# Writing out the routing stage of a mixture-of-experts layer, with its token lists built by one-hot products

## The reference

```python
x = x + mixed @ w_out[l]
h2 = rms_norm(x, norm_ffn_g[l])
...
group_p = jax.nn.softmax((ht @ rg_w + rg_b).astype(jnp.float32), axis=-1)
gp, gi = lax.top_k(group_p, 1)
...
tp, ti = lax.top_k(ep, TOP_K)
...
order = jnp.argsort(flat_e)
...
padded = ((counts + MOE_BLOCK - 1) // MOE_BLOCK) * MOE_BLOCK
...
dest = pstart[se] + (jnp.arange(A, dtype=jnp.int32) - start[se])
...
slot_tok = jnp.full((cap,), T, jnp.int32).at[dest].set(stok)
...
xb = h_pad[slot_tok].reshape(n_blocks, MOE_BLOCK, D)

def expert_block(args):
    xblk, e = args
    hid = jax.nn.silu(xblk @ w1[e]) * (xblk @ w3[e])
    return hid @ w2[e]
```

## Time and profile before

| | us |
|---|---|
| median of 3 timed runs | 4951.96 (4951.84 to 4953.2) |
| the profiled execution, as a whole | 4939.51 |
| span of its trace, first to last instruction | 4937.7 |
| PE busy in it | 4243.3 (86%) |
| DVE / ACT / POOL busy | 1567.0 / 1090.8 / 290.2 |

### The profile page before, as it was taken

The page is one execution under the profiler, slowest core; times in us unless marked ns, Lnnn a source line. Parts: engine busy times, 40 slices in busy tenths (PEclk is TensorE's granted clock), DMA queues, the critical chain, the costliest instruction groups (busy, mean ns, idle before and its releaser), DMA issues. The chain is left out here.

```text
span 4937.7 us, 63014 instructions
## 1 busy us (share of the span) xinstructions
PE 4243.3 (86%) x23058; PEld 2190.4 (44%) x23059; DVE 1567.0 (32%) x2896; ACT 1090.8 (22%) x1837; POOL 290.2 (6%) x297
## 2 busy tenths in 40 slices
PE   7899996888987849984988969999969995999996
PEld 4555445774433424442444534444434443444442
DVE  3355463542221122223165530110136536100112
ACT  1155223442100101111044300000026522000002
POOL 0000002320000010001000000000000000000000
PEclk9899998999998869997999979999989997999998
DMA  2130145432213139975001458888731133888884
GB/s 90 54 143 24 49 162 135 89 68 77 93 35 115 64 128 370 357 265 208 17 14 72 173 185 311 304 309 313 247 112 43 64 112 131 304 313 309 311 305 174
DMA packets 427020, 820.70 MB, mean 166 GB/s; under 512 B 146640, under 2 KB 288080, under 8 KB 393808
## 3 DMA queue, kind: packets, MB, share of 16 engines
q1 hardware_dynamic: 397968, 717.33, 41.9%
q0 software_dynamic: 17216, 60.83, 4.3%
q10 hardware_dynamic: 11648, 39.88, 2.0%
HBM read 692.09 MB, written 125.86 MB: 166 GB/s over the span
## 5 line engine op out<-in xcount | busy, mean ns | idle before, releaser
L2829 PE MATMUL ec1e_pg<-ec_wg,ec1e_xT 128*128 128x512 f32 x1024 | 445.2, 595 | 2.2 <-DVE ec1e_xT L2882 2.2
L2829 PE MATMUL ec0e_pg<-ec_wg,ec0e_xT 128*128 128x512 f32 x1024 | 444.5, 595 | 2.1 <-DVE ec0e_xT L2882 2.1
L2829 PEld LDWEIGHTS ec1e_pg<-ec_wg,ec1e_xT 128*128 128x128 f32 x1024 | 195.6, 191 | 249.0 <-issue 249.0
L2829 PEld LDWEIGHTS ec0e_pg<-ec_wg,ec0e_xT 128*128 128x128 f32 x1024 | 195.4, 191 | 248.3 <-issue 248.3
L1371 PE MATMUL mix_pb<-h_h_all,mix_wg 128*128 128x512 f32 x512 | 223.3, 597 | 12.2 <-DMA mix_wg<-in_w_in_dram 12.2
L1861 PE MATMUL exp_pg<-exp_wb,exp_xT 128*128 128x512 f32 x512 | 224.9, 598 | 6.4 <-DMA exp_wb<-in_w_dram 6.4
L3113 PE MATMUL lrui_pA<-lrui_xT,lrui_w 128*128 128x512 f32 x512 | 223.1, 595 | 2.6 <-ACT lrui_xT L3187 2.6
L2855 PE MATMUL ec1e_py<-lru_wd,ec1e_hidT 128*128 128x512 f32 x512 | 223.4, 594 | 0.0
L2855 PE MATMUL ec0e_py<-gqaw_wd,ec0e_hidT 128*128 128x512 f32 x512 | 223.4, 594 | 0.0
L679 PE MATMUL front_pz<-h_h_all,front_w 128*128 128x512 f32 x480 | 211.6, 599 | 8.8 <-DMA front_ones<-in_head_ones_dram 8.8
L2190 PE MATMUL gqap_pq<-gqap_w,gqap_xT 128*128 128x512 f32 x384 | 180.7, 631 | 22.4 <-DVE gqap_xT L2235 17.5
(11 more groups left out here) (533 smaller groups left out, 6135.5 us busy)
## 6 DMA issues: line engine op xcount, KB each, us to landing
ec_wg<-in_moe_w_gate_up_dram SPq DMA_DIRECT2D x256, 1024.0 KB, 6.4
exp_wb<-in_w_dram SPq DMA_DIRECT2D x64, 1024.0 KB, 15.2
gqaw_wd<-in_moe_w_down_dram SPq DMA_DIRECT2D x128, 512.0 KB, 4.4
lru_wd<-in_moe_w_down_dram SPq DMA_DIRECT2D x128, 512.0 KB, 4.4
exp_w2b<-in_w_dram SPq DMA_DIRECT2D x32, 1024.0 KB, 14.2
wkv_inp<-arrays SPq DMA_DIRECT2D x160, 128.0 KB, 3.0
arrays<-front_out SPq DMA_DIRECT2D x36, 512.0 KB, 5.7
yb<-mlaa_zero SPq DMA_DIRECT2D x1, 16384.0 KB, 52.8
```

Of the source, the lines that this page charges most:

```text
L2829: return nc.tensor.matmul(pg[:, b, :], xT[:, k, :], wg[:, k, b * HALF:(b + 1) * HALF], start=k == 0, stop=k == KD - 1)
```

## The change

Routing is written out, without loops, for all 8 tiles. `po`, `x1`, `xt`, `h2` and `h2T` exist twice and alternate by tile. The product is issued in halves with the transposes and logits of the tile before between them; the residual sum too is made in halves, each released by its own count. `mT` goes into the products directly. `mT`'s first part, `wo` and the first `x` tiles are loaded ahead of the constants. The choice of experts is made for tiles 0 to 5 inside the written-out sequence, and for tiles 6 and 7 after it.

The list of tokens is no longer scattered. For each of the 16 columns of slots DVE makes two one-hot arrays: `at_pos` (position in the block, 128 wide) and `in_block` (number of the block, 48 wide, times the token's number). 16 products on PE sum them to `pt[position, block]`, which is the list, and DVE copies it to `moe.idx`. As soon as the experts of blocks 0 and 1 are known SP loads their weights, and POOL gathers their rows, both still inside the routing phase. Buffers that both phases use belong to a new outer phase `moe`. In the experts loop SP loads the weights of the second pair of a turn and of the first pair of the next turn; POOL copies a column of `moe.idx` before each gather.

The core of the diff:

```diff
+class Moe:
...
+        self.idx = ph.sb("idx", [P, MOE_BLOCKS + 2], U32)
+        self.block_e = ph.sb("block_e", [P, MOE_BLOCKS + 2], U32)
+        self.pair_used = ph.sb("pair_used", [P, MOE_BLOCKS // 2 + 1], U32)
+        self.xg = ph.sb("xg", [P, self.R, D])
+        self.wb = [ph.sb("wb0", [P, 2, 2, KD, D_EXP]), None]
+        self.w2b = [ph.sb("w2b0", [P, 2, 2, D]), None]
+        self.wg_done = [ph.sem(f"wg_done{s}") for s in range(self.R)]
+        self.wd_done = [ph.sem(f"wd_done{s}") for s in range(self.R)]
+        self.x_in = [ph.sem(f"x_in{s}") for s in range(self.R)]
...
+    def load_gu(self, sp, s, e):
+        for n, w in enumerate((self.w1, self.w3)):
+            sp.dma_start(self.wb[s // 2][:, s % 2, n, :, :], w[0][ds(e, 1), :, :].rearrange("o (k p) f -> p (o k) f", p=P)).then_inc(self.wg_done[s], 16)
+
+    def load_dn(self, sp, s, e):
+        sp.dma_start(self.w2b[s // 2][:, s % 2, :, :], self.w2[0][ds(e, 1), :, :].rearrange("o (k p) f -> p (o k) f", p=P)).then_inc(self.wd_done[s], 16)
...
-        ident = ph.sb("ident", [P, P])
-        vec = ph.sb("vec", [P, VEC_N])
+        ident, vec = moe.ident, moe.vec
...
+        po = ph.ps("po", [P, 2, D])
...
+                mix_view = mixT_dram.rearrange("(k p) t -> p k t", p=P)
+                sp.dma_start(mT[:, :, 0:EARLY], mix_view[:, :, 0:EARLY]).then_inc(early, 16)
+                for h in range(2):
+                    sp.dma_start(wo[:, :, halves[h]], w_out[0, :, halves[h]].rearrange("(k p) n -> p k n", p=P)).then_inc(wo_in[h], 16)
+                    sp.dma_start(xt[:, h, :], x[h * P:(h + 1) * P, :]).then_inc(x_in[h], 16)
...
-                with sp.Fori(0, NT) as i:
-                    S.hold(x1_ready, last(i))
-                    sp.dma_start(xt[:, :], x[ds(i * P, P), :]).then_inc(x_in, 16)
-                    S.hold(x1_ready, now(i))
-                    sp.dma_start(x1_dram[ds(i * P, P), :], x1[:, :]).then_inc(x1_out, 16)
-                    S.hold(h2_ready, now(i))
-                    sp.dma_start(h2_dram[ds(i * P, P), :], h2[:, :]).then_inc(h2_out, 16)
-                sp.wait_ge(x1_out, 16 * (NT + 1))
-                sp.wait_ge(h2_out, 16 * (NT + 1))
-
-                sp.wait_ge(zeroed, 1)
-                sp.dma_start(slot_tok.rearrange("(p b) o -> p (b o)", p=P), zero[:, :]).then_inc(zeroed, 16)
+                for t in range(NT):
+                    u, rows = t % 2, slice(t * P, (t + 1) * P)
+                    sp.wait_ge(x1_ready, 2 * t + 2)
+                    sp.dma_start(x1_dram[rows, :], x1[:, u, :]).then_inc(x1_out[u], 16)
+                    if t + 2 < NT:
+                        sp.dma_start(xt[:, u, :], x[(t + 2) * P:(t + 3) * P, :]).then_inc(x_in[u], 16)
+                    sp.wait_ge(h2_ready, t + 1)
+                    sp.dma_start(h2_dram[rows, :], h2[:, u, :]).then_inc(h2_out[u], 16)
+                sp.wait_ge(first_e, 1)
+                for s in range(2):
+                    e = moe.expert_of(sp, s)
+                    moe.load_gu(sp, s, e)
+                    moe.load_dn(sp, s, e)
+                for u in range(2):
+                    sp.wait_ge(x1_out[u], 16 * (NT // 2))
 
...
-                    nc.gpsimd.tensor_copy(m_t[:, :, :], mT[:, :, ds(i * P, P)]).then_inc(m_in, 1)
...
-                    pool.indirect_dma_start(slot_tok, bass.IndirectOffsetOnAxis(ap=slot_u[:, n:n + 1], axis=0),
-                                            tok[:, n % NT:n % NT + 1], None).then_inc(scattered, 16)
-                pool.wait_ge(scattered, 16 * 2 * NT)
+                for u in range(2):
+                    pool.wait_ge(h2_out[u], 16 * (NT // 2))
+                pool.wait_ge(idx_ready, 1)
+                for s in range(2):
+                    pool.indirect_dma_start(moe.xg[:, s, :], None, h2_dram, bass.IndirectOffsetOnAxis(ap=moe.idx[:, s:s + 1], axis=0)).then_inc(moe.x_in[s], 16)
...
+                pe.wait_ge(early, 16)
+                for t in range(NT):
+                    if t == EARLY // P:
+                        pe.wait_ge(late, 16)
+                    product(t, 0, range(KD))
+                    if t:
+                        turn_h2(t - 1)
+                    product(t, 1, range(KD // 2))
+                    if t:
+                        logits(t - 1)
+                    product(t, 1, range(KD // 2, KD))
...
+                pe.wait_ge(in_ready, 1)
+                for j in range(2 * NT):
+                    if j % NT == 0:
+                        pe.wait_ge(pos_ready, j // NT + 1)
+                    m = nc.tensor.matmul(pt[:, 0:MOE_BLOCKS], at_pos[:, j, :], in_block[:, j, :], start=j == 0, stop=j == 2 * NT - 1)
+                m.then_inc(i_psum, 1)
...
+                def add(t, h):
+                    u = t % 2
+                    dve.wait_ge(half_psum, 2 * t + h + 1)
+                    if h == 0:
+                        dve.wait_ge(x_in[u], 16 * (t // 2 + 1))
+                        if t >= 2:
+                            dve.wait_ge(x1_out[u], 16 * (t // 2))
+                            dve.wait_ge(sq, t - 1)
+                    nc.vector.tensor_tensor(x1[:, u, halves[h]], po[:, u, halves[h]], xt[:, u, halves[h]], ALU.add).then_inc(x1_ready, 1)
...
+                def choose(a, b):
+                    s, n = slice(a, b), b - a
+                    full = [P, n, N_GROUPS, PER_GROUP]
+                    dve.wait_ge(l_kept, b)
+                    gl = lg[:, s, 0:N_GROUPS]
+                    V.link(nc.vector.reduce_max(gmax[:, s], gl, AX_X))
+                    first_of(goh[:, s, :], gl, gmax[:, s], s, n, N_GROUPS)
...
+                    for m in range(2):
+                        V.link(nc.vector.tensor_tensor(ohe[:, m, s, :, :], oh[:, m, s, :].unsqueeze(2).to_broadcast(full), group, ALU.mult))
+                    V.link(nc.vector.tensor_tensor(mem[:, s, :], ohe[:, 0, s, :, :].rearrange("p t g e -> p t (g e)"),
+                                                   ohe[:, 1, s, :, :].rearrange("p t g e -> p t (g e)"), ALU.add))
+                    for t in range(a, b):
+                        V.link(nc.vector.tensor_tensor(cum[:, t + 1, :], cum[:, t, :], mem[:, t, :], ALU.add))
...
+                add(0, 0)
+                add(0, 1)
+                for t in range(NT):
+                    norm(t)
+                    if t + 1 < NT:
+                        add(t + 1, 0)
+                    scaled(t)
+                    keep_logits(t)
+                    if t == NT - 3:
+                        choose(0, NT - 2)
+                    if t + 1 < NT:
+                        add(t + 1, 1)
+                choose(NT - 2, NT)
+                dve.sem_inc(members, 1)
                 dve.sem_inc(exp_in, 1)
...
+                experts_of(0, 2)
+                dve.sem_inc(first_e, 1)
+                V.link(nc.vector.tensor_tensor(rank[:, :, :], pr[:, 0:NT * N_EXP].rearrange("p (t e) -> p t e", e=N_EXP),
+                                               pstart[:, :].unsqueeze(1).to_broadcast([P, NT, N_EXP]), ALU.add))
+                for m in range(2):
+                    V.link(nc.vector.tensor_tensor(pick[:, m, :, :], rank[:, :, :], ohe[:, m, :, :, :].rearrange("p t g e -> p t (g e)"), ALU.mult))
+                V.link(nc.vector.tensor_reduce(slot_f[:, :].rearrange("p (m t) -> p m t", m=2), pick[:, :, :, :], AX_X, ALU.add))
+
+                wide = [P, 2 * NT, MOE_BLOCKS]
+                V.link(nc.vector.tensor_tensor(in_block[:, :, :], slot_f[:, :].unsqueeze(2).to_broadcast(wide), blocks.unsqueeze(1).to_broadcast(wide), ALU.is_ge))
+                V.link(nc.vector.tensor_reduce(base[:, :], in_block[:, :, :], AX_X, ALU.add))
+                V.link(nc.vector.tensor_scalar(base[:, :], base[:, :], float(P), float(P), ALU.mult, ALU.subtract))
+                V.link(nc.vector.tensor_tensor(pos[:, :], slot_f[:, :], base[:, :], ALU.subtract))
+                V.link(nc.vector.tensor_tensor(in_block[:, :, :], base[:, :].unsqueeze(2).to_broadcast(wide), blocks.unsqueeze(1).to_broadcast(wide), ALU.is_equal))
+                for m in range(2):
+                    mine = slice(m * NT, (m + 1) * NT)
+                    nc.vector.tensor_tensor(in_block[:, mine, :], in_block[:, mine, :],
+                                            tab[:, TAB + P:TAB + P + NT].unsqueeze(2).to_broadcast([P, NT, MOE_BLOCKS]), ALU.mult)
+                dve.sem_inc(in_ready, 1)
+                for m in range(2):
+                    mine = slice(m * NT, (m + 1) * NT)
+                    V.link(nc.vector.tensor_tensor(at_pos[:, mine, :], pos[:, mine].unsqueeze(2).to_broadcast([P, NT, P]),
+                                                   tab[:, TAB:TAB + P].unsqueeze(1).to_broadcast([P, NT, P]), ALU.is_equal))
+                    dve.sem_inc(pos_ready, 1)
+                experts_of(2, MOE_BLOCKS)
+                firsts = be_f[:, :].rearrange("p (n u) -> p n u", u=2)[:, :, 0]
```

(30 more changed lines are left out.)

341 lines of the change are left out of this document (137 added, 204 removed).

## The result

The changed kernel takes 4869.51 us (median of 4 runs, 4865.5 to 4873.35) against 4951.9 (4 runs, 4949.94 to 4953.2): ratio 0.9834, 95% interval 0.9817 to 0.9851. Five more rounds of the same kernel, on another occasion, gave 4875.19 (4873.73 to 4878.3), ratio 0.9842 (0.9828 to 0.9855). So the gain is 77 to 82 us. The prediction had 68.3, and its range began at 4870.0, half a microsecond above the first median. The direction, the closed turn at full clock and the shorter lists came as forecast. Three steps of the sum did not: the stretch from the x1 sum to h2 (which the old rows gave with two table loads in it), the addition of busy times, and the barrier hidden beside the gather.

The account below looks back on a forecast made before the run. PE bounds the experts stage, so its start matters; routing has PE idles, a lowered clock and a tail of small steps. Terms -46.1 - 5.1 - 14.8 - 3.9 + 1.6 = -68.3 us: 4871.2 profiled, 4883.7 median, range 4870 to 4902.

Parts of the forecast that it names:

- the stretch from the x1 sum to h2: Routing: 5.7 us from the sum to the end of L1665, taken from the old rows, less a 0.4 us register wait.
- the addition of busy times: Routing, PE's own work per turn: 13.7 + 1.04 (transposes) + 1.95 (logits) = 16.7 us.
- the barrier hidden beside the gather: Between routing and experts: the barrier of about 1.5 us hides beside the gather's landing.
- Start: Routing's beginning: constants moved behind mT and wo bring the first product forward, gain 5 us, bounds 4 and 6.5.
- The turn: One routing tile on PE: no idle, clock not brought down, 16.8 us instead of 23.90.
- The stall at tile 6: Routing: choose(0, 6) makes the sum late, PE idles 3.5 us and the clock falls: 6.5 us, between 3.5 and 8.
- The last tile's chain: Routing, last x1 sum to last logits kept: 13.5 us instead of 14.3, gain 0.8.
- Choice and lists: Routing's tail: last logits to ranks 8.1 us, gain 5.1; ranks to first gather 18.1 us, gain 14.8.
- To the first expert product: From the first gather's issue to the first expert product: 12.9 us instead of 16.8, gain 3.9.
- Experts: Experts stage: loop unchanged, one more barrier as phase moe closes, loss 1.6 us, bounds 0 and 3.6.
- Rival 1: Routing's turn does not close: PE waits and the clock falls in 7 turns, 25 us back, 4908; chance 0.12.
- Rival 3: Larger gain: no clock fall in the stall, one-hot products at 1.00, no exit barrier, best start: 4874; chance 0.06.

Follow-up runs that it names:

- product in one piece: Changed kernel with PE's whole product first, then transposes and logits of the tile before; combine stage's first load at 600.0 us after routing's first load, against 584.5.
- Exp before the square: Changed kernel plus an unused one-column Exp ahead of ACT's square in each routing tile; routing's first load to combine's first load 586.5 us, against 584.5.
- sums before the next product: Changed kernel with each product waiting for both x1 sums of the tile before; routing's first load to combine's first load 597.7 us, against 584.5.
- filled, choice moved: Changed kernel plus 29 unread products in PE's waits, choose(0, 6) moved behind tile 6's second half sum; 4872.58 us, ratio 0.9837 to the kernel before.
- Exp behind the square: Changed kernel plus an unused one-column Exp between ACT's square and root in each routing tile; routing's first load to combine's first load 592.6 us, against 584.5.

## Why the prediction was off

**Start** (5.0, measured 4.6): right; putting the constants back costs 3.8.

**The turn** (16.8, measured 16.4): right in kind, no idle and the clock at 1.00. The step that failed was the addition of busy times, 1.04 and 1.95, where the starts are 0.87 and 1.71 apart. Seven turns: 2.9 us.

**The stall at tile 6** (6.5, measured 0.8): the largest miss. The step was "from the sum to the end of L1665 as in the rows, 5.7": that stretch of the earlier trace rows has two table loads in it, 2.6 us, which the written-out order does not make. Measured from the end of the sum it is 2.6. The slack was therefore 3.4 us (h2 ends at 1639.83, its transposes start at 1643.22), not 0.6, the late sum (which was forecast well) cost 0.56 of idle instead of 3.5, and the clock did not fall. Where the idle was restored, it cost 3.17, and the fall 1.7 rather than 3.0.

**The last tile's chain** (gain 0.8, measured 3.8): the same two loads, 2.6 of the 3.0 us.

**Choice and lists** (5.1 and 14.8, measured 5.3 and 14.4): right, by widths of rows, and the one-hot products by the logits' row at 0.50 (7.2 for 7.03).

**To the first expert product** (3.9, measured 2.7): 12.9 forecast, 14.1 measured, that is 1.4 between the two issues, 5.7 landing, 1.7 end of phase, 5.3 transposes. The step "the barrier hides beside the gather's landing" failed: it stands behind it, 1.7 us. The 1.6 us for a slow first issue did not come (1.13 instead of 2.60), but the second issue, 1.4 us behind the first, was not in the sum. That the weights would be in time was right, and without their early issue the product comes 7.8 us later.

**Experts** (-1.6, measured +0.7): the loop gained nothing, as said. The first product took 15.21 us instead of the 16.46 of the earlier trace rows, 1.25 less, which the sum had left out; what remains is 0.6 us for the second phase's end and POOL's copies, which no run tells apart.

Together 2.9 + 5.7 + 3.0 - 0.6 (the first product with the step to its sum, 16.2 instead of 15.65) + 2.3 (experts), less 0.4 + 0.4 + 1.2 and plus 0.2 for the other parts, is the 11.5 us between 68.3 and 79.8.

**The number itself.** The 12.5 us between the profiled run and the median of before were carried over. After, the profiled run is 4866.97, 2.5 under its median; profile against profile the gain is 72.5, since the stages outside happened to be 6.6 us longer in its trace, and 0.7 more lies outside the traces. 4952.0 - 79.8 is 4872, between the two medians, so the lower end of the range, 4870, stood too close to the time. None of the prediction's three signs of being wrong came (no fall of the clock in the turns, no gather that landed behind the barrier, a pair of 23.48 us): they did not cover a stretch that was too long in the sum.

**The rivals.** Rival 1 (the turn does not close) did not come, though one piece of its mechanism is real: the product in one piece shows it in three turns. Rival 3 (more than I say) was on the right side, and two of its items came, the clock in the stall and most of the exit (0.6 us at most instead of 1.6). But its list held costs that the sum already named; the error was one inside a row that had been taken over whole. The range should have asked what in those 5.7 us belongs to the loop.

## What to carry to other kernels

Before a stretch of the old trace is reused as a duration, list every instruction in it on every engine and ask which of them the new order still makes; a table load at the head of each turn of a loop is one that writing out removed here. Add up starts, not busy times, for an engine that is always fed. A transfer that a phase's end waits for is not hidden by being issued early. A tail in which PE mostly idles had its products at a granted clock of 0.50 here; filling the waits halved the one-hot products (7.03 to 3.74 us) and brought the first gather 5.7 us forward, of which 3.5 reached the combine stage.

## What the runs showed of the hardware beyond that

A table load took 1283 ns in both kernels, and cost nothing where it stood ahead of a wait (Exp before the square). The granted clock held at 1.00 over single idles of 0.56 (after), 0.78 (sums before the next product) and 1.74 us (Exp before the square) in a full stream of products. It fell after 2.54 (filled, choice moved), 3.17 (Exp behind the square) and 4.84 us (sums before the next product), at a price of 1.7, 1.7 and 2.5 us; with 1.32 us of idle and the narrow logits behind it (product in one piece), it fell in some turns and not in others. Why it differs between those turns stays open. So does what a kernel without the barrier between the two stages would gain; it wasn't tried.
